# Output rows moved ahead of the last head's scores, and ScalarE's probability copies ahead of an exponential

## The reference

```python
def memory_cross_attention(q, mem, norm_w, w_kv):
    kv = (rms_norm(mem, norm_w) @ w_kv).reshape(bsz, m, 2, MEM_HEADS, MEM_HEAD_DIM)
    k, v = kv[:, :, 0], kv[:, :, 1]
    scores = einsum('bshd,bmhd->bhsm', qh, k) * (MEM_HEAD_DIM ** -0.5)
    p = softmax(scores, axis=-1)
    return einsum('bhsm,bmhd->bshd', p, v).reshape(bsz, s, MEM_WIDTH)

# layer 0: the mixer's result is joined with the memory heads and projected
h = h + concatenate([y, m], axis=-1) @ out_w
# layer 1: attention of 16 query heads on 4 key heads in blocks of 128 tokens
sc = einsum('bqhgd,bkhd->bhgqk', qi, ki) * scale      # masked to the window
mx = maximum(max(sc, axis=-1), sink)
p = exp(sc - mx[..., None])
denom = sum(p, axis=-1) + exp(sink - mx)
out = einsum('bhgqk,bkhd->bqhgd', p / denom[..., None], vi)
h = h + concatenate([att, m], axis=-1) @ out_w
# each layer: every token goes to 2 of 8 experts of its best group
h = h + hierarchical_moe(h, ...)                      # 32 experts, gated MLPs
```

## Time and profile before

| | |
|---|---|
| median of 3 runs | 1314.37 us (1312.51 to 1315.31) |
| the profiled execution | 1316.85 us |
| its span in the trace | 1314.9 us |
| TensorE matmul busy | 1197.8 us (91%) |
| VectorE busy | 280.6 us (21%) |
| ScalarE busy | 205.3 us (16%) |
| GpSimd busy | 32.4 us (2%) |
| DMA | 463.03 MB, mean 352 GB/s |

### The profile page before, as it was taken

The page is one execution under the profiler, slowest core; times in us unless marked ns, Lnnn a source line. Parts: engine busy times, 40 slices in busy tenths (PEclk is TensorE's granted clock), DMA queues, the critical chain, the costliest instruction groups (busy, mean ns, idle before and its releaser), DMA issues.

```text
span 1314.9 us, 15025 instructions
## 1 busy us (share of the span) xinstructions
PE 1197.8 (91%) x5996; PEld 590.6 (45%) x5996; DVE 280.6 (21%) x679; ACT 205.3 (16%) x487; POOL 32.4 (2%) x42
## 2 busy tenths in 40 slices
PE   7999999999999999989687999999999999967695
PEld 5874765444344444533232465553344444422231
DVE  5741543031111111100000336231111111100001
ACT  2223323120000000000001335221000000000002
POOL 0001210000000000000000012000000000000000
PEclk9999989999999999998888999999999999987899
DMA  9930259589999999999999771689999999999997
GB/s 355 350 128 25 49 219 386 226 313 409 406 426 427 426 427 426 424 426 425 426 426 416 293 287 65 230 318 384 416 426 427 427 427 426 426 427 426 426 427 285
DMA packets 84728, 463.03 MB, mean 352 GB/s; under 512 B 7552, under 2 KB 9648, under 8 KB 36528
## 3 DMA queue, kind: packets, MB, share of 16 engines
q1 hardware_dynamic: 84656, 462.02, 85.6%
HBM read 460.91 MB, written 1.07 MB: 351 GB/s over the span
## 4 chain that ended last, share of the span: by engine, by line
PE 68%; SPq 16%; DMA 10%; DVE 2%; ACT 2%; issue 1%; DVEq 0%; ACTq 0%
PE bank L1590 19%; PE bank L419 14%; SPq L272 14%; PE bank L1599 10%; PE bank L1563 5%; DMA h<-in_w_down 5%; PE bank L1580 5%; PE bank L402 3%; PE bank L1918 2%; DMA h<-in_w_up 2%; DMA late<-in_w_down 2%; PE bank L358 1%; SPq L1359 1%; PE bank L387 1%; PE bank L1063 1%
## 5 line engine op out<-in xcount | busy, mean ns | idle before, releaser
L1590 PE MATMUL bank<-own,work 128*64 128x512 f32 (+1 forms) x1128 | 269.4, 618 | 20.1 <-DMA own<-in_w_up 9.8
L1590 PE MATMUL bank<-late,work 128*32 128x512 f32 (+1 forms) x560 | 144.2, 621 | 12.5 <-DMA own<-in_w_up 12.5
L1599 PE MATMUL bank<-own,work 128*32 128x512 f32 (+1 forms) x464 | 124.6, 657 | 27.2 <-DMA own<-in_w_down 11.3
L1590 PEld LDWEIGHTS bank<-own,work 128*64 128x64 f32 (+1 forms) x1128 | 77.4, 127 | 148.9 <-issue 148.8
L1468 DVE TENSOR_TENSOR work<-work,bank 128x512 f32<-128x512 f32 x24 | 25.5, 1061 | 474.9 <-ACT work L1527 474.9
L1563 PEld LDWEIGHTS bank<-work,xs 128*128 128x128 f32 x768 | 90.8, 194 | 39.9 <-issue 39.9
L1563 PE MATMUL bank<-work,xs 128*128 128x128 f32 x768 | 100.0, 284 | 2.1 <-DVE work L1400 2.1
L1527 ACT ACTIVATE work<-bank 128x512 f32<-128x512 f32 x24 | 14.3, 597 | 532.0 <-PE bank L1590 532.0
L1580 PE MATMUL bank<-work 128*128 128x512 f32 x192 | 87.1, 595 | 3.1 <-DVE work L1473 1.6
L419 PE MATMUL bank<-xnT,own 128*128 128x256 f32 x384 | 84.7, 380 | 0.0
L1599 PE MATMUL bank<-late,work 128*64 128x512 f32 (+1 forms) x232 | 70.6, 726 | 9.4 <-DMA own<-in_w_down 4.2
(11 more groups left out here) (324 smaller groups left out, 1304.7 us busy)
## 6 DMA issues: line engine op xcount, KB each, us to landing
own<-in_w_up SPq DMA_DIRECT2D x78, 1024.0 KB, 26.1
own<-in_w_gate SPq DMA_DIRECT2D x63, 1024.0 KB, 25.5
own<-in_w_down SPq DMA_DIRECT2D x54, 1024.0 KB, 26.4
late<-in_w_gate SPq DMA_DIRECT2D x38, 1024.0 KB, 25.7
late<-in_w_up SPq DMA_DIRECT2D x32, 1024.0 KB, 26.3
late<-in_w_down SPq DMA_DIRECT2D x28, 1024.0 KB, 25.7
own<-in_a_in_w SPq DMA_DIRECT2D x17, 1024.0 KB, 13.5
h<-in_w_down SPq DMA_DIRECT2D x10, 1024.0 KB, 28.5
```

What stands on the lines that cost most here:

```text
L1590: ins = pe.matmul(bank[q * T:(q + 1) * T, :], self.xg[:, at:at + T], cut(tile(q), k=4)[:, k, :], start=(half == 0 and k == 0), stop=(half ...
L1599: ins = pe.matmul(self.b_down[out][q * T:(q + 1) * T, :], self.turned[:, at:at + T], cut(tile(q), j=2)[:, j, 512 * out:512 * out + 512], s ...
```

## The change

Three edits, of which the last only renames.

1. In `mixer_a` the step `outm` 0 moves from behind `pv` 2 to ahead of `sc` 3. ScalarE's last two sums of squares hang on `pT` 3 instead of `outm` 0, which keeps their place on ScalarE.
2. In `mixer_b` ScalarE walks a list of its own, `act_order`. In it an odd part `as` i (from 3 on) stands right behind `aT` i-2, instead of behind `as` i-1. The exponentials of the odd part thus come behind that turn's memory steps and behind both copies `aT`. The other engines keep `order`.
3. `SUMS` changes, since `out` 0 to 3 now take banks 4 to 7. In `mixer_b` and in the expert stages banks 4 and 5 change names.

```diff
-SUMS = [[0, 3, 4, 7], [0, 2, 5, 7]]
+SUMS = [[0, 3, 5, 7], [0, 2, 4, 7]]
...
-        order += [("mk", 3), ("pv", 1), ("pT", 2), ("sc", 3), ("pv", 2), ("outm", 0), ("pT", 3), ("outm", 1), ("pv", 3), ("outm", 2), ("outm", 3)]
+        order += [("mk", 3), ("pv", 1), ("pT", 2), ("outm", 0), ("sc", 3), ("pv", 2), ("pT", 3), ("outm", 1), ("pv", 3), ("outm", 2), ("outm", 3)]
...
-        squares_at = {("yd", 5): [0, 1, 2], ("yd", 6): [3, 4], ("yd", 7): [5], ("outm", 0): [6, 7]}
+        squares_at = {("yd", 5): [0, 1, 2], ("yd", 6): [3, 4], ("yd", 7): [5], ("pT", 3): [6, 7]}
...
+        act_order = [key for key in order if key[0] != "as" or key[1] == 1 or key[1] % 2 == 0]
+        for i in range(3, NA, 2):
+            act_order.insert(act_order.index(("aT", i - 2)) + 1, ("as", i))
...
-            for key in order:
+            for key in act_order:
```

## The result

The changed kernel takes 1318.9 us in the median of 20 runs (1313.44 to 1322.21). The kernel before took 1314.78 us beside it (20 runs, 1312.51 to 1318.29). The ratio is 1.0023, with a 95% interval of 1.0015 to 1.0031: 3.0 us slower, between 2.0 and 4.1. The medians themselves lie 4.1 apart, at the upper end of that interval. The forecast was +2.0. The profiled execution took 1320.67 us for a span of 1318.9, 4.0 us more than the span of before.

What follows compares the result with a forecast made beforehand. Neither mixer's time was taken as hidden by the DMA-bound parts, with TensorE the bound at the first mixer's end. +2.3 (first edit) and -0.3 (second) made +2.0 on 1314.37: 1316.4 us, range 1313.0 to 1319.0.

Steps and rivals of the forecast that it cites:

- The forecast proper: Whole kernel: the likeliest outcome, +2.0 us to 1316.4 us, own range 1315.3 to 1317.5, chance 0.40.
- the rival of the clock: First mixer: TensorE's clock falls behind the new wait in most executions, +3.6 us, 1318.0 us; chance 0.28.
- The dry queue: Both mixers: the DMA queue runs dry, so a stall ahead of these points moves all that follows by its full length.
- The case in which the edits don't reach the end: Rival: the DMA-bound parts take the shifts up, 1314.4 us; chance 0.07.
- First edit, the wait: End of the first mixer: TensorE waits 2.27 us ahead of `pT` 3 for the softmax `outm` 0 had covered; taken as +2.3.
- The clock behind that wait: First mixer, behind `pT` 3's wait: a clock fall would cost 1.6 us, chance somewhat less than half, left out of the sum.
- the likeliest sum: Whole kernel: +2.3 for the first mixer, -0.3 for the second, no clock fall, +2.0 us in all.
- Second edit, what it moves and what becomes late: Second mixer: `av` 0.47 us earlier per turn, but VectorE's division waits for GpSimd, so turns take 10.44 us instead of 9.99.
- The short turn: Second mixer, rival: VectorE's division isn't held up by GpSimd, -2.2 there, +0.1 in all, 1314.5 us; chance 0.18.
- Second edit, the sum: Second mixer: the last turn's gain of 2.0 nearly used up by 1.8 lost ahead; -0.3 us, bounds -3.8 and +0.5.
- The sum: Whole kernel: +2.3 first mixer, -0.3 second, nothing for names; +2.0 on the median 1314.37 gives 1316.4 us.

Runs made afterwards that it cites:

- e6: Against the kernel before: only the first edit, with three useless matmuls (512, 512, 256 columns) filling TensorE's wait ahead of `pT` 3; ratio 1.0017.
- e6b: Repeat of e6, the first edit with three useless matmuls in the wait, against the kernel before; ratio 1.0026.
- e9: Against the kernel before: both edits, with VectorE doing `memory_softmax` ahead of the second `inverse`; ratio 0.9993.
- e1: Against the kernel before: only the first edit with its bank names, ScalarE's order in the second mixer as before; ratio 1.0024.
- e1b: Repeat of e1, the first edit alone, against the kernel before; ratio 1.0032.
- e3: Against the kernel before: only the second edit, with VectorE doing `memory_softmax` ahead of the second `inverse`; ratio 0.9978.
- e5: Against the kernel before: only the second edit, with GpSimd's work on odd parts 9, 11, 13 held until VectorE's division is through; ratio 0.9959.
- e5b: Repeat of e5, the second edit with GpSimd's later start, against the kernel before; ratio 0.9970.
- e8: Against the kernel before: e3 plus ScalarE's copies `aT` ahead of the exponentials of `sc` 2 and 3, `rows0` 3 later; ratio 0.9970, 1312.29 us.
- the filled kernels: First edit with useless matmuls put into TensorE's wait ahead of `pT` 3, against the kernel before: e6 and e6b, ratios 1.0017 and 1.0026.
- e2: Against the kernel before: only the second edit (ScalarE's own order in the second mixer); ratio 1.0001.
- e2b: Repeat of e2, the second edit alone, against the kernel before; ratio 0.9995.

## Why the prediction was only half right

The forecast proper, 1315.3 to 1317.5 us with a chance of 0.40, wasn't met: the time lies 0.1 under the end of the whole range (1319.0), in the rival of the clock (0.28), and slower than before by just more than the 0.2% that counted as a difference.

**The dry queue.** Right. The stretch between the two distances keeps its length but for one gather in e6 and e6b, and e9 shows both stages' shifts, +4.12 and -2.18. The case in which the edits don't reach the end is out by the medians: e1 and e1b are slower, e3, e5, e5b and e8 faster, each by more than its interval.

**First edit, the wait.** Right. The forecast was a wait of 2.27 us, released by L1211. It was 2.38, and 2.46 in the first distance. That 2.27 was also the idle time of the earlier trace rows is a coincidence of two unlike waits. The estimate of 0.15 us from a release to TensorE's next start stands in the chain as 0.14.

**The clock behind that wait.** This is the step that failed. Its price was right: 1.6 against the 1.69 measured. Its chance was put at "somewhat less than half", and it was left out of the sum. The profiles with the wait show it three times in four. The dense `outm` work on both sides, which I took as a protection, didn't protect. The row that did bear on it was the wait of 2.27 us at 184.88, and I named it myself: a wait as long as one that was punished. That row repeats: the fall is there in all 14 profiles. The likeliest sum should have been +3.6. What the fall costs in the median isn't settled by the filled kernels, since theirs fell at the first gather.

**Second edit, what it moves and what becomes late.** The mechanism was right in each link. `sc`'s exponential stands directly ahead of `aT`. The division meets GpSimd's scaling each time and waits for it: 1.43 us, ending 0.55 behind GpSimd (0.54 forecast). The turns of the changed kernel were 10.47 and 10.86 against 10.44. The short turn without the shared time was priced at 9.64 and -2.2 us, and e5 gave 9.73 and 2.0 less than before in the second distance. Only it doesn't come by itself: GpSimd was first each time.

**Second edit, the sum.** +0.2 instead of -0.3, inside the bounds. I had forecast how late VectorE's turn starts, but didn't draw from it that the wait ahead of `av` 4 would grow. VectorE's start at 804.76 in e2 is 0.9 us late when set against the start of the mixer, as forecast (805.4 against 804.55), and `av` follows it. So TensorE waited 1.96 to 1.98 us there, and the clock fell behind that in all three profiles of this order (changed, e2, e2b). VectorE bounds these turns, so only part of the fall counts: in e2 it waited 0.33 us for TensorE, and in the changed kernel the copies `aT` of the next turn came late. Either way the two turns took 21.3 us instead of the 20.9 forecast, and that is the 0.5 by which the sum was off. The last `av` had no wait, as forecast, and started 5.1 us into its turn, as forecast.

**The sum.** By the profiles: 2.46 for the wait, 1.69 if the fall comes in three of four executions, 0.2 for the second mixer, 3.9 in all. Four profiles are few for that share. The ratio gives 3.0 (2.0 to 4.1). The time of 1318.9 us lies nearest to the rival of the clock (1318.0), not to the forecast. Of the distance to either, 0.4 us is the kernel before, whose median was 1314.78 in the longer comparison and not 1314.37.

## What to carry to other kernels

When an edit takes the cover from a wait, add the clock to its price: if the trace shows one idle time of the same length with slow matmuls behind it, count that fall in the likeliest sum. Take its price from all the slow work behind it, and not from one group of rows. When an instruction is moved behind another on one engine, look at what stands behind the instruction that now waits: the division behind the late `inverse` ate the gain, and putting it ahead gave 0.22%. If two engines slow each other at one point, move the one that nobody waits for.

## What the runs showed of the hardware

- TensorE idle for 2.38 us, with dense 128x512 work ahead and behind, was followed by a fall of the clock in 3 of 4 profiles, for 1.66 to 1.69 us lost each time. Idle times of 2.25 to 2.56 us some 20 us earlier were followed by one in 14 of 14, for 1.7 or 3.3 us. Those of 0.8 to 1.4 us ahead of `av` had none behind them. With 2.31 us of useless matmuls in the place of the 2.38 there was no fall (2 profiles), but one came at the first gather, for 1.5 and 2.8 us. The Trainium skill ("TensorE: Matmul & The Clock Gate", "The HAM clock gate") says that how many matmuls are hit varies from run to run, and the profiles of one kernel (e1 and e1b) agree.
- The second gather takes 2.02 us in five profiles (e2, e3, e5, e5b, e9) and 2.90 to 3.65 in the nine others, behind the same wait of 1.04 us. With the matmuls behind it the fall costs 1.2 to 1.6 us in six of them and 2.85 in three.
- The division with two SBUF inputs took 1.43 us beside a GpSimd instruction of 1.04 that began 0.16 earlier, and 0.69 alone. VectorE's L2098 in e5, which reads one of its inputs from PSUM (`bank`), began at 813.89 and took 0.69 us with GpSimd at work from 814.00, and GpSimd's instruction took its 1.04 us too:

```profile
814.00 1.04 POOL L1835 TENSOR_TENSOR late<-late,work 128x512 f32<-128x512 f32 x1 [3.35 <-DVE late L2047]
```

- A float32 matmul over 512 columns stands in the trace as two passes of about 0.43 us, so it takes twice what one record suggests.
